# Expert stage of an encoder layer: u rows asked for one position ahead, interleaved with v rows; both halves of a quad's v products behind tiles 0, 1 and 4, 5

## The chip, the cores and the metric

The kernel runs on one core of one Trainium2 chip. The metric is the device time of one execution in microseconds, the median of several runs. The core has TensorE (PE, with its weight loads PEld), VectorE (DVE), ScalarE (ACT), GpSimd (POOL), SyncE (SP) and 16 DMA engines that serve all queues. Inputs and outputs lie in device memory (HBM).

## What is computed

One layer of a bidirectional encoder on 1024 tokens of width 1024. A token-mixing half (attention and spatial gating) comes first, then a channel-mixing half, PEER: each token picks 128 of 16384 single-neuron experts (8 heads, top 16 each), and

```python
u = exp_u[ib]                                             # (tokens, 128, 1024)
a = jax.nn.gelu(jnp.einsum('td,ted->te', xb, u)) * gb
y = jnp.einsum('te,ted->td', a, exp_v[ib])                # 128 rows of v per token
```

The change lies in the last large stage, the one that forms y.

## The kernel before

The stage is the method `experts`. It treats the two halves of the 1024 tokens in two ways at once.

**Dense half (512 tokens).** All 16384 experts are applied, with the gate zero where an expert isn't chosen. The experts come in 128 chunks of 128; a loop over 128 *positions* j takes one chunk each (`chunk_of[j]`). For a chunk, SP loads the gates g, the hidden values h (or they are computed here, see `up`) and 128 rows of v (L2156, L2158, L2161). DVE multiplies g by h (L2346). ACT makes a high part of the product and of v (L2234, L2236), DVE the low parts (L2356 and L2360). PE works on a *pair* of positions: 8 output tiles n = 0 to 7, each 6 matmuls of 128x512 (three products for each of the two positions), and DVE adds each tile to y (`add`, L2323). A tile's PSUM bank is one of four, so tile n waits for the sum of tile n - 4. PE begins a pair when both positions' low parts are ready (`a_split`, `v_split`). In the first 88 positions, 64 chunks also need their hidden values: `up` runs 24 matmuls for one chunk, up(m + 3) behind tile 1 of each pair and up(m + 4) behind tile 6 of 20 of the 44 pairs, with its own split of u on ACT (L2217) and DVE (L2332).

**Gathered half (4 blocks of 128 tokens).** Here the chosen experts are fetched row by row. POOL issues indirect DMAs, each of 128 rows of 1024 f32 (512 KB). For the first factor, one DMA brings one u row for each of 128 tokens, into one of U_RING = 4 slots (L2184), and one custom DVE instruction multiplies it with the tokens and sums (`dot`, L2316). There are 352 such dots, DOTS = 4 for each of the first 88 positions. For the second factor, position m covers a *quad* of 4 tokens: four DMAs, one for each of LANES = 4, bring all 128 v rows of a token (L2194) into one of V_RING = 2 sets of slots. PE multiplies them with the gates held in `ex_spread` (`mix(m, half)`, L2420): 4 matmuls for each half of the width, 128x32 by 128x512. When half 1 is done, `mixed` counts up.

**What sets the order.** Each engine runs its own hand-written order. On POOL, for each position j: four u rows of position j (each waits until the slot's last dot is done: `dotted`), then a wait until `mixed` has reached j - 1, then four v lanes of position j:

```python
def fetch_v(m):
    r = m % V_RING
    if m >= V_RING:
        pool.wait_ge(mixed, m - V_RING + 1)
    for lane in range(LANES):
...
for j in range(C):
    if j < DOT_CHUNKS:
        for i in range(DOTS):
            fetch_u(EARLY_DOTS + j * DOTS + i)
    fetch_v(j)
```

On DVE, position j is: g*h, sum of a tile, dot 0, low part of the activations, sum, low part of v, dot 1, (low part of u), sum, dot 2, sum, dot 3. The sums of position j are those of the pair before: tiles 0 to 3 where j is even, 4 to 7 where it is odd. On PE, the four `mix` calls of a pair (positions m and m + 1, halves 0 and 1) stand behind tiles 1, 3, 5 and 7. All DMAs that POOL issues go through one queue in order (q0); SP and ACT have queues of their own. A few steps come once per 32 positions: `fetch_u` loads the next block's tokens on POOL's queue (L2183), and `row_out`, `turn_row` and `space` carry a block's result out of PSUM and its gates into `ex_spread`.

Of the kernel before, what the change touches and what calls it, by code (L numbers as in the profile page):

```python
# [49 lines left out]
EARLY_DOTS = 160  # L50
# [6 lines left out]
class Layer:  # L57
# [1995 lines left out]
    def experts(self, h2_hi, h2_lo, y, expert_at, expert_of, weight_of, dots):  # L2053
# [11 lines left out]
        DOTS = P // SEG  # L2065
        DOT_CHUNKS = (NG * P - EARLY_DOTS) // DOTS
        DOT_PAIRS = DOT_CHUNKS // 2
        FUSED = C - EARLY_UPS
        LANES = 4
        U_RING, V_RING = 4, 2  # L2070

        chunk_of, up_at, up_of = [], [], {}
        for pair in range(C // 2):
            twice = (pair + 1) * (FUSED - DOT_PAIRS) // DOT_PAIRS > pair * (FUSED - DOT_PAIRS) // DOT_PAIRS
            for i in range(2):
                j = 2 * pair + i
# [23 lines left out]
        v_got = [self.sem(f"ex_v_got{i}") for i in range(V_RING)]  # L2100
# [20 lines left out]
        with ExitStack() as c:  # L2121
# [5 lines left out]
            v_rows = self.sb(c, "ex_v_rows", [P, V_RING * LANES, D])  # L2127
# [19 lines left out]
            with nc.Block() as block:  # L2147
# [23 lines left out]
                @block.gpsimd  # L2171
                def _(pool):
                    every_v = a["peer_v"].rearrange("i j d -> (i j) d")
                    every_u = self.u_rows.rearrange("i j d -> (i j) d")

                    def fetch_u(n):
                        r, i = n % U_RING, n - EARLY_DOTS
                        if i >= U_RING:

                            pool.wait_ge(dotted, i - U_RING + 1)  # L2180
                        if n % P == U_RING - 1 and n // P > 1:

                            pool.dma_start(rows, self.h2_scr[n // P].rearrange("p (h n) -> p h n", h=2)).then_inc(next_rows_loaded, 16)  # L2183
                        pool.indirect_dma_start(u_rows[:, r], None, every_u,  # L2184
                                                bass.IndirectOffsetOnAxis(ap=expert_at[:, n // P, n % P:n % P + 1], axis=0)).then_inc(u_got[r], 16)

                    def fetch_v(m):
                        r = m % V_RING
                        if m >= V_RING:

                            pool.wait_ge(mixed, m - V_RING + 1)
                        for lane in range(LANES):
                            t = lane * 32 + m % 32
                            pool.indirect_dma_start(v_rows[:, r * LANES + lane], None, every_v,  # L2194
                                                    bass.IndirectOffsetOnAxis(ap=expert_of[:, m // 32, t:t + 1], axis=0)).then_inc(v_got[r], 16)

                    for j in range(C):
                        if j < DOT_CHUNKS:
                            for i in range(DOTS):
                                fetch_u(EARLY_DOTS + j * DOTS + i)  # L2200
                        fetch_v(j)

                @block.scalar
                def _(act):
# [170 lines left out]
                @block.tensor  # L2375
                def _(pe):
                    def turn_gates(b):
                        pe.wait_ge(gated, b + 1)
                        if b >= 2:

                            pe.wait_ge(row_placed, 2 * (b - 1))
                        pe.transpose(gate_ps, curve[:], self.ident[:]).then_inc(gates_turned, 1)

                    def turn_row(b, half):
                        pe.wait_ge(row_copied, b + 1)

                        pe.wait_ge(gates_held, min(b + 2, NG))
                        if half:

                            pe.wait_ge(row_placed, 2 * b + 1)  # L2390
                        for k in range(4):
                            at = (4 * half + k) * P
                            last = pe.transpose(turn_ps[:, k * P:(k + 1) * P], row[:, at:at + P], self.ident[:])
                        last.then_inc(row_turned, 1)

                    def up(j):
                        if j not in up_of:
                            return
                        i = up_of[j]
                        pe.wait_ge(u_split, i + 1)  # L2400
                        if i:

                            pe.wait_ge(gelu_done, i)
                        for k in range(KT):
                            part, cols = k // 4, slice((k % 4) * P, (k % 4 + 1) * P)
                            last = self.product3(pe, hid, u_hi[i % 2][:, part, cols], u_lo[i % 2][:, part, cols], h2_hi[:, k, 0:HALF], h2_lo[:, k, 0:HALF],
                                                 k == 0, k == KT - 1)
                        last.then_inc(hidden, 1)

                    def mix(m, half):  # L2410
                        r, at = m % V_RING, m % 32
                        if half == 0:
                            pe.wait_ge(v_got[r], 16 * LANES * (m // V_RING + 1))
                            if at % SPAN == 0:
                                pe.wait_ge(spaced, m // SPAN + 1)
                            if at == 0 and m:
                                pe.wait_ge(row_copied, m // 32)
                        for lane in range(LANES):
                            first = 32 * (lane * SPAN + at % SPAN) + on - at
                            last = pe.matmul(ps[lane * 32:(lane + 1) * 32, 4 + half], spread[:, first:first + 32],  # L2420
                                             v_rows[:, r * LANES + lane, half * HALF:(half + 1) * HALF], start=at == 0, stop=at == 31)
                        if half == 1:
                            last.then_inc(mixed, 1)
                    turn_gates(0)
                    for j in range(3):
                        up(j)
                    for pair in range(C // 2):
                        m = 2 * pair
                        if m and m % SEG == 0:
                            turn_gates(m // SEG)  # L2430
                        pe.wait_ge(a_split, 2 * pair + 2)
                        pe.wait_ge(v_split, 2 * pair + 2)
                        for n in range(KT):
                            d = slice(n * P, (n + 1) * P)
                            if pair or n >= 4:

                                pe.wait_ge(added, pair * KT + n - 3)
                            for i in range(2):
                                ring = (2 * pair + i) % 4
                                last = self.product3(pe, ps[:, n % 4], v_hi[:, ring, d], v_lo[:, ring, d], act_hi[ring], act_lo[ring],  # L2440
                                                     i == 0, i == 1)
                            last.then_inc(summed, 1)
                            if n % 4 == 0 and m and m % SEG == 0:
                                turn_row(m // SEG - 1, n // 4)
                            if n % 2:
                                mix(m + n // 4, n // 2 % 2)
                            if n == 1:
                                up(m + 3)
                            if n == 6:
                                up(m + 4)  # L2450
                    turn_row(NG - 1, 0)
                    turn_row(NG - 1, 1)
# [59 lines left out]
```

## Time and profile before

| | us |
|---|---|
| median of 3 runs | 5116.48 (5108.94 to 5135.47) |
| the profiled execution | 5122.61 |
| its span | 5121.0 |
| PE, DVE, ACT, POOL busy in the span | 3897.4, 3018.5, 1490.2, 1250.4 |
| stage `experts`, first to last g*h on DVE | 3291.86 to 5043.14 |

The profile's page gives busy times of engines, the span in 40 slices (128 us each) with the rate of the DMAs, and groups of instructions. "Idle before" names what ended the idle time of an engine; for POOL, "issue" is a fixed gap in which it waits for nothing that is shown. The granted clock of TensorE is given as a share of 2.4 GHz. In the timeline, PE's ends are modelled and overlap the next start, so start to start is the time that a matmul takes.

### The profile page before, as it was taken

How to read it: one execution, taken by the hardware profiler on the slowest of the kernel's cores; microseconds unless marked ns; L12 is line 12 of the kernel's file. 1: busy time of each engine (PE TensorE's matmuls, PEld its weight loads, DVE VectorE, ACT ScalarE, POOL GpSimd, SP SyncE). 2: the span in 40 equal slices, each digit the busy share in tenths (PEclk: the TensorE clock that was granted, in tenths of full speed). 3: DMA queues.
4: the chain of work that ended last, by engine and by line, in shares of the span. 5: the costliest groups of instructions: out<-in, count | busy, mean ns of one | idle time of the engine just before them, and what ended most of it. 6: DMA issues, size and time to landing. Idle time of an engine off the chain costs nothing. (4 is left out here: it accounts for less than half of the span.)

```text
span 5121.0 us, 51116 instructions
## 1 busy us (share of the span) xinstructions
PE 3897.4 (76%) x17580; PEld 2820.9 (55%) x17580; DVE 3018.5 (59%) x5900; ACT 1490.2 (29%) x2161; POOL 1250.4 (24%) x1080
## 2 busy tenths in 40 slices
PE   2899898798866977696654567587888788788886
PEld 1666665577655766585443455355555555555553
DVE  5666665112243322597999957766666666666555
ACT  3444443333332123212566521111111111111111
POOL 0000000000001000000000057655555555555442
PEclk9999897799987987798766688788889898998997
DMA  3000000577843346102322399999999999999996
GB/s 125 19 23 26 17 23 7 199 254 276 286 165 125 107 147 226 45 29 74 105 70 72 111 337 368 355 338 335 343 338 344 345 349 334 339 345 331 342 353 242
DMA packets 386986, 1058.67 MB, mean 207 GB/s; under 512 B 33776, under 2 KB 102768, under 8 KB 383600
## 3 DMA queue, kind: packets, MB, share of 16 engines
q0 software_dynamic: 153504, 567.35, 29.5%
q1 hardware_dynamic: 185568, 351.11, 20.3%
q10 hardware_dynamic: 47728, 137.91, 7.3%
q8 instruction: 96, 1.57, 0.1%
q14 instruction: 90, 0.74, 0.0%
HBM read 905.76 MB, written 150.47 MB: 206 GB/s over the span
## 5 line engine op out<-in xcount | busy, mean ns | idle before, releaser
L2194 POOL DMA_INDIRECT ex_v_rows<-peer_v_dram,expert_of x512 | 609.5, 1190 | 649.2 <-PE psum L2420 504.4
L2316 DVE CUSTOM_DVE_ANT_1 ex_u_rows<-ex_u_rows,y 128x1024 f32<-128x1024 f32 x352 | 428.5, 1218 | 498.1 <-DMA ex_u_rows<-u_rows_scratch,expert_at 480.5
L382 PE MATMUL psum<-in_hi,v_hi 128*128 128x512 f32 x1024 | 462.8, 452 | 278.1 <-DVE v_lo L2360 134.3
L382 PE MATMUL psum<-in_hi 128*128 128x512 f32 x1024 | 440.7, 430 | 99.3 <-DVE in_lo L1913 52.3
L382 PEld LDWEIGHTS psum<-in_hi,v_hi 128*128 128x128 f32 x1024 | 212.5, 208 | 504.1 <-issue 378.9
L2323 DVE TENSOR_TENSOR y<-y,psum 128x512 f32<-128x512 f32 x512 | 349.0, 682 | 169.6 <-PE psum L384 159.0
L383 PE MATMUL psum<-in_lo,v_hi 128*128 128x512 f32 x1024 | 434.1, 424 | 0.0
L384 PE MATMUL psum<-in_hi,v_lo 128*128 128x512 f32 x1024 | 432.8, 423 | 0.0
L383 PE MATMUL psum<-in_lo,in_hi 128*128 128x512 f32 x1024 | 423.6, 414 | 0.0
L384 PE MATMUL psum<-in_hi,in_lo 128*128 128x512 f32 x1024 | 422.7, 413 | 0.0
L2184 POOL DMA_INDIRECT ex_u_rows<-u_rows_scratch,expert_at x352 | 378.2, 1074 | 150.6 <-issue 103.7
L2234 ACT ACTIVATE in_hi<-g 128x512 fp32r<-128x512 f32 x128 | 80.9, 632 | 1115.1 <-DVE g L2346 1074.8
L1036 POOL DMA_DIRECT2D gates_ada<-w_adaT_dram x16 | 8.7, 543 | 1432.0 <-PEq L521 930.3
L382 PEld LDWEIGHTS psum<-in_hi 128*128 128x128 f32 x1024 | 207.8, 203 | 184.4 <-issue 77.2
L1763 POOL DMA_INDIRECT sc_cand<-u_rows_scratch,expert_at x108 | 145.4, 1346 | 661.2 <-DVE expert_of L1866 582.7
L2420 PE MATMUL psum<-ex_v_rows,ex_spread 128*32 128x512 f32 x2048 | 275.0, 609 | 38.7 <-DMA ex_v_rows<-peer_v_dram,expert_of 34.8
L2040 PE MATMUL psum<-sc_w_hi,sc_second 128*128 128x128 f16 x512 | 101.2, 287 | 228.9 <-DVE sc_second L1892 228.9
L384 PEld LDWEIGHTS psum<-in_hi,v_lo 128*128 128x128 f32 x1024 | 212.9, 208 | 51.6
L383 PEld LDWEIGHTS psum<-in_lo,v_hi 128*128 128x128 f32 x1024 | 214.6, 210 | 39.3
L384 PEld LDWEIGHTS psum<-in_hi,in_lo 128*128 128x128 f32 x1024 | 206.9, 202 | 46.8
L383 PEld LDWEIGHTS psum<-in_lo,in_hi 128*128 128x128 f32 x1024 | 207.5, 203 | 38.1
L382 PE MATMUL psum<-in_hi,front_w_hi_t 128*128 128x512 f32 x512 | 216.3, 422 | 15.4 <-DVE front_w_lo_t L479 15.4
(357 smaller groups left out, 8636.7 us busy)
## 6 DMA issues: line engine op xcount, KB each, us to landing
y<-peer_v_dram SPq DMA_DIRECT2D x128, 512.0 KB
front_r_in<-peer_uT_dram SPq DMA_DIRECT2D x96, 512.0 KB
u_rows_scratch<-front_r_out ACTq DMA_DIRECT2D x96, 512.0 KB, 3.8
sc_u_raw<-peer_uT_dram SPq DMA_DIRECT2D x64, 512.0 KB
route_scratch<-sc_stage SPq DMA_DIRECT2D x32, 1024.0 KB, 10.5
g<-route_scratch SPq DMA_DIRECT2D x128, 256.0 KB
front_w_raw<-w_in_dram SPq DMA_DIRECT2D x32, 512.0 KB, 6.2
gates_ada<-w_adaT_dram POOLq DMA_DIRECT2D x16, 1024.0 KB
```

The source lines that it names most:

```text
L382: pe.matmul(out, w_hi, x_hi, start=start, stop=False)
L383: pe.matmul(out, w_hi, x_lo, start=False, stop=False)
L384: return pe.matmul(out, w_lo, x_hi, start=False, stop=stop)
L1036: pool.dma_start(ada[:, s], a["w_adaT"][:, bass.ds(at[s], 2), :]).then_inc(ada_loaded[s], 16)
L1763: pool.indirect_dma_start(u_rows[r], None, every_u, bass.IndirectOffsetOnAxis(ap=expert_at[:, n // P, n % P:n % P + 1], axis=0)).then_inc( ...
L2040: pe.matmul(to, second[:, s, tok], w_hi[:, s, tok], start=True, stop=False)
L2184: pool.indirect_dma_start(u_rows[:, r], None, every_u, bass.IndirectOffsetOnAxis(ap=expert_at[:, n // P, n % P:n % P + 1], axis=0)).then_i ...
L2194: pool.indirect_dma_start(v_rows[:, r * LANES + lane], None, every_v, bass.IndirectOffsetOnAxis(ap=expert_of[:, m // 32, t:t + 1], axis=0) ...
L2234: act.activation(act_hi[ring], g[:, s], ACT.Copy).then_inc(a_hi_done, 1)
L2316: dve.tensor_tensor_reduce(out=halves(u_rows[:, r]), in0=halves(u_rows[:, r]), in1=rows, scale=1.0, scalar=0.0, op0=ALU.mult, op1=ALU.add, ...
L2323: dve.tensor_tensor(to, to, ps[:, n % 4], ALU.add).then_inc(added, 1)
L2420: last = pe.matmul(ps[lane * 32:(lane + 1) * 32, 4 + half], spread[:, first:first + 32], v_rows[:, r * LANES + lane, half * HALF:(half + 1 ...
```

## The change

Two edits. On POOL, the four u rows of position 0 are issued first; then, at position j, one u row of position j + 1 and one v lane of position j alternate. The wait for `mixed` stands before lane 0, behind the first u row. On PE, `mix(m, 0)` and `mix(m, 1)` stand behind tiles 0 and 1, `mix(m + 1, 0)` and `mix(m + 1, 1)` behind tiles 4 and 5.

```diff
-                    def fetch_v(m):
-                        r = m % V_RING
-                        if m >= V_RING:
+                    def fetch_v(m, lane):
+                        r, t = m % V_RING, lane * 32 + m % 32
+                        if lane == 0 and m >= V_RING:
 
                             pool.wait_ge(mixed, m - V_RING + 1)
-                        for lane in range(LANES):
-                            t = lane * 32 + m % 32
-                            pool.indirect_dma_start(v_rows[:, r * LANES + lane], None, every_v,
-                                                    bass.IndirectOffsetOnAxis(ap=expert_of[:, m // 32, t:t + 1], axis=0)).then_inc(v_got[r], 16)
-
+                        pool.indirect_dma_start(v_rows[:, r * LANES + lane], None, every_v,
+                                                bass.IndirectOffsetOnAxis(ap=expert_of[:, m // 32, t:t + 1], axis=0)).then_inc(v_got[r], 16)
+
+                    for i in range(DOTS):
+                        fetch_u(EARLY_DOTS + i)
                     for j in range(C):
-                        if j < DOT_CHUNKS:
-                            for i in range(DOTS):
-                                fetch_u(EARLY_DOTS + j * DOTS + i)
-                        fetch_v(j)
+
+                        for i in range(DOTS):
+                            if j + 1 < DOT_CHUNKS:
+                                fetch_u(EARLY_DOTS + (j + 1) * DOTS + i)
+                            fetch_v(j, i)
...
-                            if n % 2:
-                                mix(m + n // 4, n // 2 % 2)
+                            if n % 4 < 2:
+                                mix(m + n // 4, n % 4)
```

Sizes of the rings, the number and size of the DMAs and all arithmetic stay as they were.

## Rows read from the trace of the kernel before

**Rows 1.** The page: the span, and the rate of the DMAs by slice.

```profile
span 5121.0 us, 51116 instructions
...
GB/s 125 19 23 26 17 23 7 199 254 276 286 165 125 107 147 226 45 29 74 105 70 72 111 337 368 355 338 335 343 338 344 345 349 334 339 345 331 342 353 242
```

**Rows 2.** The timeline of DVE: g*h of positions 0, 88 and 127.

```profile
3291.86 0.63 DVE L2346 SCALAR_TENSOR_TENSOR g<-g,h 128x512 f32<-128x512 f32 x1
...
4689.23 0.68 DVE L2346 SCALAR_TENSOR_TENSOR g<-g,h 128x512 f32<-128x512 f32 x1
...
5043.14 0.68 DVE L2346 SCALAR_TENSOR_TENSOR g<-g,h 128x512 f32<-128x512 f32 x1
```

**Rows 3.** Windows: stretch, its us, busy by engine, PE clock, DMA share, GB/s.

```profile
3292.00:4689.00 1397.00, 1118.92 (x4996) 746.72 (x4995) 894.94 (x1375) 242.94 (x324) 807.89 (x698) 0.89 0.93 342
4689.00:5043.00 354.00, 317.28 (x1560) 187.24 (x1559) 198.47 (x276) 65.42 (x88) 165.66 (x152) 0.97 0.94 341
3089.00:3250.00 161.00, 113.83 (x408) 87.07 (x408) 123.56 (x194) 24.94 (x33) 122.79 (x88) 0.87 0.97 365
3905.00:3931.00 26.00, 15.77 (x63) 10.63 (x64) 17.78 (x29) 4.10 (x5) 17.99 (x15) 0.80 1.00 384
3931.00:3938.00 7.00, 7.00 (x34) 4.58 (x32) 7.00 (x12) 1.02 (x2) 1.96 (x3) 1.00 0.72 225
```

**Rows 4.** Waits from 3292 to 4689: us in total, times, longest.

```profile
DVE ex_u_rows L2316 <- DMA ex_u_rows<-u_rows_scratch,expert_at: 480.5, 85, 10.7
...
POOL ex_v_rows L2194 <- PE psum L2420: 348.0, 62, 9.4
```

**Rows 5.** Waits from 4689 to 5043, the same columns.

```profile
POOL ex_v_rows L2194 <- PE psum L2420: 151.2, 37, 10.6
...
PE psum L2420 <- DMA ex_v_rows<-peer_v_dram,expert_of: 32.8, 20, 2.6
```

**Rows 6.** Timeline, early part: two mixes on PE, and the v lane POOL issues next.

```profile
4081.89 1.06 PE L2420 MATMUL psum<-ex_v_rows,ex_spread 128*32 128x512 f32 x8
...
4091.25 1.07 PE L2420 MATMUL psum<-ex_v_rows,ex_spread 128*32 128x512 f32 x8
...
4092.62 0.94 POOL L2194 DMA_INDIRECT ex_v_rows<-peer_v_dram,expert_of  x1 [8.61 <-PE psum L2420]
```

**Rows 7.** Groups of instructions from 3292 to 5043: busy, mean ns, idle before.

```profile
L2194 POOL DMA_INDIRECT ex_v_rows<-peer_v_dram,expert_of x500 | 597.5, 1195 | 641.0 <-PE psum L2420 499.2 <-issue 140.5 <-remote 1.3
...
L2316 DVE CUSTOM_DVE_ANT_1 ex_u_rows<-ex_u_rows,y 128x1024 f32<-128x1024 f32 x352 | 428.5, 1218 | 498.1 <-DMA ex_u_rows<-u_rows_scratch,expert_at 480.5 <-DMA y<-token_rows_scratch 17.6
...
L2184 POOL DMA_INDIRECT ex_u_rows<-u_rows_scratch,expert_at x348 | 374.5, 1076 | 140.5 <-issue 102.8 <-DVE dots L2316 37.7
L2323 DVE TENSOR_TENSOR y<-y,psum 128x512 f32<-128x512 f32 x500 | 340.7, 681 | 154.4 <-PE psum L384 145.4 <-issue 5.9
...
L2360 DVE TENSOR_TENSOR v_lo<-y,v_hi 128x1024 fp32r<-128x1024 f32 x127 | 155.6, 1225 | 0.0
```

**Rows 8.** Timeline: a u row's issue on POOL, and the dot that waited for it.

```profile
3909.80 0.94 POOL L2184 DMA_INDIRECT ex_u_rows<-u_rows_scratch,expert_at  x1 [0.30 <-issue]
...
3915.84 1.23 DVE L2316 CUSTOM_DVE_ANT_1 ex_u_rows<-ex_u_rows,y 128x1024 f32<-128x1024 f32 x1 [5.95 <-DMA ex_u_rows<-u_rows_scratch,expert_at]
```

**Rows 9.** Timeline, late part: mixes on PE.

```profile
4805.74 1.07 PE L2420 MATMUL psum<-ex_v_rows,ex_spread 128*32 128x512 f32 x8
...
4809.70 1.06 PE L2420 MATMUL psum<-ex_v_rows,ex_spread 128*32 128x512 f32 x8
...
4819.69 1.07 PE L2420 MATMUL psum<-ex_v_rows,ex_spread 128*32 128x512 f32 x8 [2.02 <-DMA ex_v_rows<-peer_v_dram,expert_of]
```

**Rows 10.** Timeline, late part: the first and last of four v lanes on POOL.

```profile
4807.11 0.94 POOL L2194 DMA_INDIRECT ex_v_rows<-peer_v_dram,expert_of  x1 [6.08 <-PE psum L2420]
...
4810.84 1.60 POOL L2194 DMA_INDIRECT ex_v_rows<-peer_v_dram,expert_of  x1 [0.30 <-issue]
```

## The prediction

> **What bounds the kernel now.** The page first: of a span of 5121.0 us, the 13 full slices from 3328 us on all lie between 331 and 353 GB/s, whatever the engines do in them [rows 1]. That is the stage `experts`. Its length is read from DVE's g*h [rows 2]: positions 0 to 88 take 1397.4 us, so a pair takes 31.76 us (44 pairs, with u rows); positions 88 to 127 take 353.9 us, so a pair takes 18.15 us (19.5 pairs, v rows alone). The windows [rows 3] show what each pair costs each engine in the first part: PE 1118.92 / 44 = 25.4 us at a granted clock of 0.89, DVE 894.94 / 44 = 20.3 us, POOL 807.89 / 44 = 18.4 us and 16 gaps of 0.30 us [rows 8], 23.2 us. None fills 31.76. The DMA engines are busy 93%. They move 342 x 1397 / 44 = 10.86 MB a pair.
>
> But the rate isn't steady. From 3905 to 3931, where POOL's queue is fed all the time, it is 384 GB/s at a share of 1.00; in the 7 us behind that, 225 [rows 3]. The waits say why: POOL waits 348.0 us, 62 times, for a mix on PE before it may ask for v rows, while DVE waits 480.5 us for u rows that stand behind those v rows in the same queue [rows 4]. One case: a mix(m, 0) starts at 4081.89, mix(m, 1) only at 4091.25, since an `up` and two tiles (36 matmuls, 8.3 us, 0.231 us each) stand between; POOL idles 8.61 us and issues at 4092.62 [rows 6]. So the bound is DMA with holes that the order of PE's work makes.
>
> **Edit 1, mixes on PE.** Count and cost stay. Two tiles and a mix take 3.96 us, so a tile is (3.96 - 1.06) / 2 = 1.45 us [rows 9]. `mixed` for an even position now comes behind tile 1, not 3: two tiles and an `up` (24 x 0.231 = 5.5 us) earlier, 8.4 us. For an odd position, behind tile 5, not 7: 2.9 us earlier, 8.4 where the pair has a second `up` (20 of 44). POOL's waits average 348.0 / 62 = 5.6 us, so most of them end at once. The other side: mix(m, 0) needs its v rows one tile (1.45 us) earlier, and what is queued behind its wait on PE is tile 1 and up(m + 3). The gates in `ex_spread` are wanted a tile earlier too, 16 times: 0 to 16 x 1.45 = 23 us. I take 0: ACT is busy 242.94 of 1397 us [rows 3] and what it waits for, `mixed`, comes earlier by more.
>
> **Edit 2, POOL's order.** The same 864 DMAs on the same queue. A u row is asked for as soon as the dot of the position before frees its slot, so it has nearly a whole position (14.7 us) for the 5.1 us from the end of its issue to its dot [rows 8], and no longer stands behind a wait for `mixed` (three of four do, but behind a wait that edit 1 ends). The 480.5 us of DVE should fall to what the DMA rate itself makes. The price: v lane i of position j now stands behind u row i of position j + 1, hence behind dot i of position j. From the end of dot 3: u issue 0.30 + 1.08, v issue 0.30 + 1.20 [rows 7, 8], 2.9 us, and then the landing, 5.1 us for the u row above and 4819.69 - 4812.44 = 7.25 us for a v lane of the late part [rows 9, 10]: the last lane is there 8.0 to 10.2 us behind dot 3. PE wants it no sooner than g*h, two sums, a dot and two low parts of DVE's next position (3 x 0.68 + 1.22 + 0.68 + 1.23 = 5.2 us, the activations' low part taken as one sum [rows 7]) and tile 0, 6.6 us. So PE may wait up to 3.6 us at mix(m, 0). It has 29.4 - 25.4 = 4.0 us to spare in a pair of the length forecast below. I cost it at nothing; without that cover it is 44 x 3.6 = 158 us. Smaller matters: the token load on POOL's queue (17.6 us of DVE's wait in all now [rows 7]) waits for the same dot as before, bounds 0 and another 17.6, taken as 0; v lanes of position 0 start behind the first dots (up to 5.3 us late), and the last mix ends up to 2.9 us sooner: taken as 0 together.
>
> **POOL as a cover.** Just ahead of the stage, with DVE busy 77%, a gather holds POOL 122.79 / 88 = 1.40 us [rows 3], against 1.20 and 1.08 in the stage [rows 7]. With DVE busier after the change, 16 x (1.40 + 0.30) = 27.2 us a pair, still under 29.4, but the margin is thin.
>
> **The rate, and the sum.** What remains is the DMA rate. Bounds: 342 (nothing filled) and 384 (no hole, over 26 us). The longest fed stretch is 3089 to 3250, 365 GB/s at a share of 0.97; scaled to 1.00 it is 376 [rows 3]. I take 370, nearest to that row. First part: 31.76 x 342 / 370 = 29.36 us, 2.40 us less, x 44 = 106 us. Late part: the ring of v slots sets it now. From the end of one mix(m, 1), 0.3 us to the issue, 5.3 us for four lanes (4807.11 to 4812.44), 7.25 us to the landing: 12.9 us; the rest of the pair, 2 tiles and 2 mixes behind it, is 5.0 us, together 17.9 against 18.15 seen [rows 9, 10]; POOL waits 151.2 us for mixes here, and PE 32.8 us for v rows [rows 5]. With the change one tile less is outside the ring: 16.5 us. By rate it is 18.15 x 341 / 370 = 16.7 us, which ends last: 1.42 x 19.5 = 28 us. PE alone needs 4 x 3.96 = 15.8. Sum: 134 us. Profiled execution 5122.6 - 134 = 4989 us; the median of the runs lies 6.1 us below it, so **4983 us**.
>
> **Rival 1, a lower ceiling of the DMAs.** If the rate is set by the mix of row gathers and block loads of this stage, no long stretch of it will pass 353 GB/s, the best full late slice [rows 1]; then 31.76 x 342 / 353 = 30.77 (44 us) and 17.53 (12 us) give 5061 us. For it: 13 slices of such even height. Against it: 384 over 26 us inside the stage, and 365 over 161 us [rows 3]. The Trainium skill, DMA: Bandwidth & Descriptors (Where 436 GB/s comes from), says that transfers between HBM and SBUF are bound by about 358 GB/s for a core; by that figure the sum would be about 79 us and the time about 5037. The same page's measured section says that a core alone on its pair goes higher, and this trace, with 365 and 384, sides with that.
>
> **Rival 2, a new wait for the old.** v lanes behind the dots leave POOL idle as long as before, only for `dotted` instead of `mixed`; the holes move and the pair stays at 31.8 us: 5116 us. For it: POOL already waits 37.7 us for dots [rows 7]. Against: dots are late now because of the u rows, and these come a position ahead.
>
> **Rival 3, slower: the last v lane closes a loop.** Dot 3 of position m, issue of the last lane (2.9 us), landing L, then on PE mix, tile 1, mix, `up`, tile 2 (1.06 + 1.45 + 1.06 + 5.5 + 1.45 = 10.5 us), then DVE's third sum of position m + 2, dot 2, sum, dot 3 (3.8 us): 17.2 + L per pair. It decides only from L = 31.76 - 17.2 = 14.6 us on; now L is 5.1 to 7.25. A u row and a v lane are issued together behind each dot, so the queue before the last lane gets longer; with L = 17 the pair is 34.2 us, + 107 us, less 28 in the late part: 5195 us. Against it: L would have to double, and one lane is 512 KB, 1.4 us at 370 GB/s, so five more would have to stand before it.
>
> **How the numbers follow.** Forecast 0.58, rival 1 0.20, rival 2 0.13, rival 3 0.09. 0.5% is 26 us, about what a measurement of this kernel can tell from no change. The first two cases are faster: 0.78; the third is the same: 0.13; the last slower: 0.09. Range: the low end is 384 GB/s throughout (28.29 us, 153 us; 16.5 us by the ring, 32 us: 4931), with 16 us more for a PE clock that rises from 0.89; the high end takes in rival 1 and part of rival 2: 4915 to 5105.
>
> **What would show it.** Right: windows of both parts at 365 GB/s or more and a share over 0.97; 29 to 29.7 us between every second g*h; POOL's wait for L2420 well under 150 us in the first part; DVE's wait for u rows under 250 us; PE waiting for v rows at L2420 at most 3 us each time. Rival 1: shares near 1 and 350 to 358 GB/s. Rival 2: POOL's wait for dots over 250 us. Rival 3: PE's waits for v rows over 5 us each, and DVE waiting for PE at its sums. I am wrong altogether if the rate stays at 342 with POOL hardly waiting.

## The result, and the profile after

The changed kernel takes 4926.32 us (median of 4 runs, 4921.15 to 4932.57), against 5117.1 us before. The ratio is 0.9623, 95% interval 0.9595 to 0.9651: 3.8% faster, a gain of 191 us where 134 were forecast. The profiled execution took 4932.57 us. First the page of the changed kernel: its span, and the rate of the DMAs by slice.

```profile
span 4930.9 us, 51116 instructions
...
GB/s 130 20 20 26 24 17 11 126 247 250 295 290 103 102 78 207 158 55 21 82 116 100 59 92 353 370 355 386 383 384 396 386 397 378 402 390 382 373 374 248
```

Where the slices stood at 331 to 353 GB/s before [rows 1], they are at 373 to 402 now. The timeline of DVE has g*h of positions 0, 88 and 127 again:

```profile
3297.88 0.63 DVE L2347 SCALAR_TENSOR_TENSOR g<-g,h 128x512 f32<-128x512 f32 x1
...
4523.31 0.68 DVE L2347 SCALAR_TENSOR_TENSOR g<-g,h 128x512 f32<-128x512 f32 x1
...
4855.94 0.68 DVE L2347 SCALAR_TENSOR_TENSOR g<-g,h 128x512 f32<-128x512 f32 x1
```

Against [rows 2] the first part fell from 1397.4 to 1225.4 us, a pair from 31.76 to 27.85; the late part from 353.9 to 332.6, a pair from 18.15 to 17.06. That is 172 + 21 us; the stage began 6 us later and what follows position 127 took 3 us less. Together 190 us, the difference of the spans. The windows (stretch, its us, busy by engine, PE clock, DMA share, GB/s):

```profile
3298.00:4523.00 1225.00, 1081.30 (x4991) 708.77 (x4989) 899.46 (x1375) 243.18 (x324) 851.66 (x702) 0.93 1.01 388
4523.00:4856.00 333.00, 312.07 (x1567) 183.55 (x1568) 202.37 (x277) 65.42 (x88) 162.28 (x156) 0.99 0.99 370
3089.00:3250.00 161.00, 120.47 (x432) 92.70 (x432) 125.30 (x197) 25.89 (x34) 129.01 (x89) 0.86 0.99 374
```

Each engine's busy time in the first part is what it was within some 6% [rows 3]: POOL's rose from 807.89 to 851.66 us, and PE's fell from 1118.92 to 1081.30 us at a granted clock of 0.93, against 0.89. The DMA share went from 0.93 to 1.01. No work went away, only holes. Now the waits of the first part (us in total, times, longest):

```profile
DVE y L2324 <- PE psum L384: 244.7, 78, 6.0
...
POOL ex_u_rows L2184 <- DVE dots L2317: 173.2, 61, 12.6
...
PE psum L2421 <- DMA ex_v_rows<-peer_v_dram,expert_of: 131.3, 28, 9.2
...
DVE ex_u_rows L2317 <- DMA ex_u_rows<-u_rows_scratch,expert_at: 58.0, 50, 3.9
...
POOL ex_v_rows L2192 <- PE psum L2421: 17.0, 13, 2.0
```

and of the late part:

```profile
POOL ex_v_rows L2192 <- PE psum L2421: 131.0, 38, 6.3
...
PE psum L2421 <- DMA ex_v_rows<-peer_v_dram,expert_of: 21.9, 21, 3.0
```

Against [rows 4], POOL's wait for mixes fell from 348.0 to 17.0 us, and DVE's wait for u rows from 480.5 to 58.0. Three waits have come up: PE for v rows, 131.3 us, where the kernel before has none in this part; DVE behind it, which now waits 244.7 us for PE at its sums (1.0 before); and POOL for dots, 173.2 us (37.7 before). One such case in the timelines of POOL and PE:

```profile
3900.82 0.94 POOL L2184 DMA_INDIRECT ex_u_rows<-u_rows_scratch,expert_at  x1 [0.31 <-issue]
3902.07 1.44 POOL L2192 DMA_INDIRECT ex_v_rows<-peer_v_dram,expert_of  x1 [0.30 <-issue]
...
3912.92 1.94 PE L2421 MATMUL psum<-ex_v_rows,ex_spread 128*32 128x512 f32 x8 [6.21 <-DMA ex_v_rows<-peer_v_dram,expert_of]
```

The lane issued until 3903.51 is the fourth of its position. PE's wait for it ends at 3912.92, 9.4 us later; PE stands idle for 6.21 us with tile 1 and an `up` queued behind the mix. Over the 28 waits of the first part, the time from the end of the fourth lane's issue to the mix that waited for it is 5.8 to 10.5 us, 8.5 us on average.

### The profile page after: what moved, and what is told of

The parts are those of the page before. It is cut to its first block and busy times, and to the rows that moved or that the text cites. A ratio compares the mean times of both kernels' runs of the same rounds, so it can differ in the third digit from the quotient of the medians.

```text
span 4930.9 us, 51116 instructions
## 1 busy us (share of the span) xinstructions
PE 3863.2 (78%) x17580; PEld 2786.9 (57%) x17580; DVE 3026.2 (61%) x5900; ACT 1490.5 (30%) x2161; POOL 1288.2 (26%) x1080
## 5 line engine op out<-in xcount | busy, mean ns | idle before, releaser
L2192 POOL DMA_INDIRECT ex_v_rows<-peer_v_dram,expert_of x512 | 621.5, 1214 | 295.1 <-PE psum L2421 150.9
L2184 POOL DMA_INDIRECT ex_u_rows<-u_rows_scratch,expert_at x352 | 400.2, 1137 | 273.4 <-DVE dots L2317 173.2
L382 PE MATMUL psum<-in_hi,v_hi 128*128 128x512 f32 x1024 | 437.0, 427 | 10.5 <-DVE v_lo L2361 7.2
L2421 PE MATMUL psum<-ex_v_rows,ex_spread 128*32 128x512 f32 x2048 | 295.2, 651 | 155.6 <-DMA ex_v_rows<-peer_v_dram,expert_of 154.7
L383 PE MATMUL psum<-in_lo,v_hi 128*128 128x512 f32 x1024 | 411.1, 401 | 0.0
L384 PE MATMUL psum<-in_hi,v_lo 128*128 128x512 f32 x1024 | 409.6, 400 | 0.0
L382 PEld LDWEIGHTS psum<-in_hi,v_hi 128*128 128x128 f32 x1024 | 197.8, 193 | 244.3 <-issue 147.8
L384 PEld LDWEIGHTS psum<-in_hi,v_lo 128*128 128x128 f32 x1024 | 198.6, 194 | 45.6
L2040 PEld LDWEIGHTS psum<-sc_w_hi,sc_second 128*128 128x128 f16 x512 | 66.0, 131 | 276.1 <-DVE sc_second L1892 276.1
```

Source lines behind the costliest of these rows:

```text
L382: pe.matmul(out, w_hi, x_hi, start=start, stop=False)
L383: pe.matmul(out, w_hi, x_lo, start=False, stop=False)
L384: return pe.matmul(out, w_lo, x_hi, start=False, stop=stop)
L2040: pe.matmul(to, second[:, s, tok], w_hi[:, s, tok], start=True, stop=False)
L2184: pool.indirect_dma_start(u_rows[:, r], None, every_u, bass.IndirectOffsetOnAxis(ap=expert_at[:, n // P, n % P:n % P + 1], axis=0)).then_i ...
```

## Experiments

Ratios are against the kernel before, run on the same chip. A pair's length is read from g*h as above, in one profiled execution of each kernel. The experiments have labels, e1 to e15; "after" in their expectations is the changed kernel.

**The two edits apart.** e1 is the mix edit alone, on the kernel before:

```diff
-                            if n % 2:
-                                mix(m + n // 4, n // 2 % 2)
+                            if n % 4 < 2:
+                                mix(m + n // 4, n % 4)
```

> Only the new places of the mixes on PE; POOL's order as before. Theory A (the gain is holes in the DMA stream, made mostly by the late `mixed`): POOL's wait for mixes in the first part falls from 348 us to under 120, the rate rises to about 370 GB/s, the time falls by 100 to 140 us, 4980 to 5015 us; the late part has all of its gain, a pair of about 17.1 us. Theory B (u rows that stand behind v rows are the cause, whoever releases them): DVE's wait for u rows stays over 350 us and the time falls by 20 to 60 us, 5055 to 5095 us, the late part's 21 us most of it.

Measured: 4902.66 us, ratio 0.9572 (0.9540 to 0.9605). Windows of both parts, then waits of the first:

```profile
3293.00:4486.00 1193.00, 1086.19 (x4999) 709.40 (x4997) 897.73 (x1378) 243.12 (x324) 827.36 (x698) 0.94 1.03 401
4486.00:4829.00 343.00, 315.03 (x1560) 184.90 (x1561) 201.75 (x275) 65.41 (x88) 161.07 (x155) 0.98 0.95 352
```

```profile
DVE ex_u_rows L2316 <- DMA ex_u_rows<-u_rows_scratch,expert_at: 248.9, 81, 4.6
...
POOL ex_u_rows L2184 <- DVE dots L2316: 160.5, 138, 8.0
...
POOL ex_v_rows L2194 <- PE psum L2420: 45.8, 54, 1.6
```

The rate is 401 GB/s, a pair of the first part takes 27.10 us, and there is no wait of PE for v rows in the list. Theory A holds for the first part, and the gain is half again as large as it said; the late part has only half of its gain (17.60 us a pair, not 17.1). This edit alone wins 216 us, more than both together. The two ratio intervals overlap slightly, so the stage is the better witness: from g*h of position 0 to that of 127 it is 1535.9 us here and 1558.1 in the changed kernel. DVE still waits 248.9 us for u rows, four times as long as in the changed kernel, and the kernel is faster all the same: that wait isn't what bounds.

e2, the POOL edit alone, is the changed kernel with the old `mix` lines.

> Only POOL's new order; the mixes stay behind tiles 1, 3, 5, 7. Theory A: POOL still waits for `mixed` before lane 0 and now holds u rows 1 to 3 of the next position behind that wait too, yet they have a position to spare; 5050 to 5085 us, late part 18.1 us a pair as before. Theory B: nearly the whole gain of the first part without any of the late part's, 4945 to 4975 us.

Measured: 5038.01 us, 0.9840 (0.9795 to 0.9884), 12 us under the range of theory A, far from theory B. A pair of the first part takes 29.73 us, a late pair 18.28. Its window and waits of the first part:

```profile
3302.00:4610.00 1308.00, 1109.29 (x4998) 731.87 (x4996) 908.17 (x1376) 243.36 (x324) 827.00 (x702) 0.92 0.96 364
```

```profile
POOL ex_v_rows L2192 <- PE psum L2421: 265.6, 61, 9.1
...
PE psum L2421 <- DMA ex_v_rows<-peer_v_dram,expert_of: 165.8, 45, 6.9
```

So of the medians (before 5117 to 5119): mixes alone -216, POOL alone -81, both -191. The second edit, as it stands, is a gain only without the first.

**Release or need?** In the changed kernel the slots are both needed and released earlier. In e3, made from the changed kernel, the halves are side by side too, but behind tiles 2, 3 and 6, 7:

```diff
-                            if n % 4 < 2:
-                                mix(m + n // 4, n % 4)
+                            if n % 4 >= 2:
+                                mix(m + n // 4, n % 4 - 2)
```

> As after, but both halves side by side behind tiles 2, 3 and 6, 7, so that `mixed` comes as late as before while the v rows are needed later. If the earlier `mixed` is what counts (theory A), about e2's time, within 15 us, and a late pair near 18.1 us. If it is the pairing of the halves that counts (v slots held for a shorter stretch between half 0 and half 1), near the time of after, 4925 to 4950 us. In the late part the distance from the end of mix(m, 1) to mix(m + 2, 0) is 7 tiles and 2 mixes as in after, so the ring would allow 16.5 us there: by that working a late pair is 17.1 us, and 20 us of the gain remain.

Measured: 4919.13 us, 0.9599 (0.9568 to 0.9631), a pair of 27.91 us and a late one of 16.96. That is not e2's time but that of the changed kernel, which speaks against theory A as I had put it. The waits of the first part point at a reason:

```profile
POOL ex_v_rows L2192 <- PE psum L2421: 168.5, 53, 7.9
...
PE psum L2421 <- DMA ex_v_rows<-peer_v_dram,expert_of: 94.8, 38, 5.7
```

Under POOL's new order there are two losses, POOL's wait for the release and PE's wait for late v lanes (265.6 and 165.8 us in e2). Both are smaller here. A reading that fits, though e3 alone doesn't show it: half 0 behind tile 2 runs after up(m + 3), so PE has more to do before it needs the lanes; and as PE then waits less before half 1, the release comes sooner too. To see the release alone, e9 has the same places with POOL's order of before, where PE has no wait for v rows in the list of the first part:

> POOL's order of before; mixes side by side behind tiles 2, 3 and 6, 7. The slots are released at the same place of PE's program as before, only half 0 comes later. Theory A (the release is what makes the holes): POOL's wait for mixes stays over 300 us in the first part, 31 to 32 us a pair, and only the late part gains its 20 us: 5090 to 5110 us. Theory E (the first part gains when no `up` stands between the halves, for whatever reason, as e3 against e2 suggests with 119 us): 4900 to 4930 us.

Measured: 5093.86 us, 0.9949 (0.9931 to 0.9968). Windows, and POOL's wait in the first part:

```profile
3290.00:4690.00 1400.00, 1121.86 (x4997) 748.11 (x4996) 896.09 (x1376) 242.64 (x324) 812.25 (x698) 0.90 0.93 341
4690.00:5013.00 323.00, 308.49 (x1560) 180.80 (x1558) 195.46 (x277) 65.46 (x88) 165.88 (x152) 1.00 1.00 375
```

```profile
POOL ex_v_rows L2194 <- PE psum L2420: 350.4, 64, 9.4
```

Theory A: 31.81 us a pair as before, 341 GB/s against 342, the same wait, and only the late part gains (16.55 us, the shortest so far). With POOL's order of before it is the release that counts. e10, made from the kernel before, leaves the mixes behind tiles 1, 3, 5, 7 and moves what stood in front of the release:

```diff
-                            if n == 1:
+                            if n == 3:
                                 up(m + 3)
-                            if n == 6:
+                            if n == 7:
                                 up(m + 4)
```

> POOL's order and the mixes' tiles (1, 3, 5, 7) of before; only the two `up` calls move behind tiles 3 and 7, behind the mixes. The halves stay apart by a tile or two, the release comes 5.5 us earlier where an `up` stood between. Theory A: 5.5 of the 8.4 us of an even position are won, POOL's wait for mixes falls by 150 us or more, first part 28.5 to 29.5 us a pair, late part unchanged at 18.1: 5000 to 5030 us. Theory E gives about the same for the first part. If only halves side by side help: 5100 to 5120 us.

Measured: 4962.03 us, 0.9697 (0.9678 to 0.9716), 38 us under the range of theory A: 28.14 us a pair at 386 GB/s, the late part hardly changed (18.37). The windows' row and POOL's wait:

```profile
3275.00:4513.00 1238.00, 1082.69 (x4998) 723.83 (x4996) 896.03 (x1376) 243.52 (x324) 830.08 (x698) 0.93 1.00 386
```

```profile
POOL ex_v_rows L2194 <- PE psum L2420: 130.2, 76, 4.3
```

With every mix behind its old tile, the `up` calls out of the way win 161 us. The halves needn't be neighbours. This run alone doesn't part theories A and E, since the `up` no longer stands between the halves either; e9 does, and there the release, left late, kept the pair at 31.81 us.

**POOL's order.** With the mixes as in the changed kernel, three other orders. e4 has first four u rows of the next position, then four lanes:

```diff
-                        for i in range(DOTS):
-                            if j + 1 < DOT_CHUNKS:
-                                fetch_u(EARLY_DOTS + (j + 1) * DOTS + i)
-                            fetch_v(j, i)
+                        if j + 1 < DOT_CHUNKS:
+                            for i in range(DOTS):
+                                fetch_u(EARLY_DOTS + (j + 1) * DOTS + i)
+                        for i in range(DOTS):
+                            fetch_v(j, i)
```

> As after, but at each position first the four u rows of the next position, then the four v lanes, instead of one of each by turns. If the alternation matters (the last v lane only 2.9 us behind the last dot, the first ones earlier), all four lanes come behind dot 3, the last at least 3 x 1.5 us later, PE's wait for v rows grows from 136 us to over 250 and the time is 20 to 60 us over after, 4945 to 4985 us. If only asking ahead matters, within 10 us of 4926.

Measured: 5023.76 us, 0.9817 (0.9781 to 0.9852), about 97 us over the changed kernel, far more than expected; a pair takes 30.11 us. Waits of the first part:

```profile
POOL ex_u_rows L2184 <- DVE dots L2318: 350.6, 139, 12.4
...
PE psum L2422 <- DMA ex_v_rows<-peer_v_dram,expert_of: 211.3, 48, 8.8
```

All lanes now stand behind dot 3. POOL idles for dots as long as it once did for mixes, and PE waits for v rows 48 times in 44 pairs, as in rival 3's loop. e5 alternates, but with u rows of the same position (no four rows up front, `fetch_u(EARLY_DOTS + j * DOTS + i)` before `fetch_v(j, i)`):

> The new places of the mixes, and POOL alternates u row i and v lane i of the same position (not one ahead). Mix edit alone gave 4903 with u first and then v; after, which asks u one position ahead, 4926, with 131 us of PE waiting for v rows. Theory C (v lanes behind the dots of their own position are what POOL's edit costs): here v lane i of position j stands only behind dot i of position j - 1, so PE's wait for v rows is under 30 us, but u rows 1 to 3 come up to three lanes later than in the mix edit alone; 4900 to 4920 us. Theory D (the alternation is what costs, since it spreads the last v lane): 4920 to 4945 us with PE's wait for v rows over 80 us.

Measured: 5021.55 us, 0.9790 (0.9764 to 0.9817); both theories missed. A pair takes 30.01 us. Waits of the first part:

```profile
DVE ex_u_rows L2315 <- DMA ex_u_rows<-u_rows_scratch,expert_at: 368.2, 189, 6.1
...
POOL ex_v_rows L2192 <- PE psum L2419: 307.6, 82, 9.2
...
PE psum L382 <- DVE v_lo L2359: 172.2, 23, 11.1
```

PE has no wait for v rows in the list, as theory C has it, but u rows 1 to 3 are now behind the wait for `mixed` and needed at once; PE waits 172.2 us for DVE's low parts, and the release comes late with it. Of these orders, alternating pays only with the u rows ahead, and u rows ahead only with the alternation.

e7 is the changed kernel with the two calls of the inner loop exchanged, the v lane first:

> As after, but v lane i comes ahead of u row i of the next position, so it stands behind dot i - 1 and not dot i, and lane 0 behind no dot of its own position. Theory C (PE's wait for v rows, 131 us, comes of lanes behind dots): that wait falls under 60 us and the time to 4900 to 4915. But u row 0 of the next position is now behind the wait for `mixed`, as in e5: if that costs more, the time is over 4930 and DVE's wait for u rows is over 150 us instead of 58.

Measured: 4893.44 us, 0.9546 (0.9521 to 0.9571), clear of the changed kernel's interval; a pair takes 26.95 us. Waits of the first part:

```profile
DVE ex_u_rows L2317 <- DMA ex_u_rows<-u_rows_scratch,expert_at: 152.8, 112, 3.9
...
POOL ex_u_rows L2184 <- DVE dots L2317: 117.5, 84, 11.4
...
PE psum L2421 <- DMA ex_v_rows<-peer_v_dram,expert_of: 47.8, 26, 5.2
```

Theory C holds, with a time 7 us below its range: one place in the queue takes PE's wait from 131.3 to 47.8 us and 44 x 0.90 = 40 us off the first part. DVE's wait for u rows did pass the 150 us that was to go with a loss, and there was none.

**Is the rate the bound now?** The page of the mix-only kernel (e1) has this rate by slice (122.6 us each):

```profile
GB/s 131 20 20 26 21 20 11 112 252 258 287 298 112 94 77 208 169 56 21 82 116 70 64 118 315 380 356 404 402 400 403 399 398 401 403 402 365 371 336 256
```

The nine full slices of its first part are even, 398 to 404 GB/s; those of the changed kernel range from 378 to 402. e11 is the mix edit alone with less to load. It reads only the first two blocks of v for the dense half and leaves out the rest, and with them SP's and ACT's waits for those blocks:

```diff
-                        if j >= 2:
-                            sp.wait_ge(v_split, j - 1)
-                        sp.dma_start(v_raw[s], ...
+                        if j < 2:
+                            sp.dma_start(v_raw[s], ...
...
-                        act.wait_ge(v_loaded[s], 16 * (j // 2 + 1))
+                        act.wait_ge(v_loaded[s], 16)
```

> The mix edit alone, without the block loads of v for the dense half from position 2 on (the first two blocks are used again and again): 1.05 of 10.8 MB a pair less. It leaves that part of the input out. If the DMA rate is what bounds the first part now (399 GB/s at a share of 1.02), a pair falls from 27.1 us to 9.76 / 0.399 = 24.5 us and the time by 90 to 120 us, 4785 to 4815 us. If PE's order and its waits bound it (PE busy 91%), by less than 40 us. In the late part the ring of v slots bounds: no more than 20 us in either case.

Measured: 4818.86 us, 0.9415 (0.9388 to 0.9442). Windows of both parts:

```profile
3283.00:4423.00 1140.00, 1069.82 (x5008) 703.24 (x5011) 898.81 (x1378) 243.36 (x324) 848.48 (x698) 0.96 0.99 378
4423.00:4733.00 310.00, 306.45 (x1554) 181.42 (x1547) 201.89 (x276) 65.46 (x88) 161.60 (x155) 1.00 0.94 327
```

It falls between the two readings. A pair goes from 27.10 to 25.91 us, not to 24.5. So fewer bytes help, and with the even slices this speaks for the rate as the bound of the mix-only kernel's first part, but something else is at most 1.2 us behind it. PE, then busy 1069.82 / 1140 = 94%, is the nearest candidate; the DMA share is still 0.99 there, and no run separates the two. The late pair goes from 17.60 to 15.89, the 15.8 us of PE's own work that the prediction gave. That is 33 us where at most 20 were expected: the ring holds the landing of the lanes, which fewer bytes may shorten, so bytes and ring weren't apart as the expectation had them.

**Putting the parts together.** e12 has mixes behind tiles 0, 1 and 4, 5 up to position 87, behind 2, 3 and 6, 7 from there on, with POOL's order of before:

```diff
-                            if n % 2:
-                                mix(m + n // 4, n // 2 % 2)
+                            late = 2 if m >= DOT_CHUNKS else 0
+                            if late <= n % 4 < late + 2:
+                                mix(m + n // 4, n % 4 - late)
```

> POOL's order of before; mixes behind tiles 0, 1 and 4, 5 for positions 0 to 87, behind tiles 2, 3 and 6, 7 from 88 on. If the parts add up: first part 27.1 us a pair (as the mix edit alone), late part 16.6 us (as e9), 4883 us, 20 us under the mix edit alone. If e9's late part owes its speed to how it is entered, the late pair stays near 17.6 us and the time near 4903.

Measured: 4884.14 us, 0.9524 (0.9499 to 0.9550); 27.20 and 16.62 us a pair, as expected. e14 adds one u row ahead of the wait (`fetch_u(EARLY_DOTS)` up front, and `range(1, DOTS + (j + 1 < DOT_CHUNKS))` for the rows of a position):

> As the kernel with two places of the mixes, with only u row 0 of the next position asked for ahead of the wait for `mixed`: dot 0 stands before the low parts on which PE's next pair waits. If the DMA rate (401 GB/s, share 1.03) bounds the first part, nothing: within 8 us of the other. If PE's waits at the start of a pair still count, 10 to 25 us less. All four v lanes come behind dot 0 of their own position, which costs if PE then waits for v rows.

Measured: 4864.85 us (4857.05 to 4882.0), 0.9494 (0.9466 to 0.9521), the fastest of the kernels that compute all of y. But its first part is shorter by 4 us only (27.11 us a pair), the late one by 5 us (16.35), and in its profile the stage began 10 us sooner, in code that is the same. From g*h of position 0 to the end of the span it is 1588.2 us against 1597.1. That fits the rate as the bound of the first part, and by these traces 9 of the 19 us between the medians are all that can be owed to this edit. Last, e15, the v lane first with the two places:

> POOL's order with the v lane first, and the late mixes behind tiles 2, 3 and 6, 7. If both gains hold and add up: first part 26.95 us a pair, late part 16.4 to 16.6 instead of 17.1, 10 to 14 us under the v-first kernel (4893): 4879 to 4884 us. If the rate has nothing left and the late part depends on how it is entered: within 5 us of 4893.

Measured: 4877.39 us (4859.22 to 4883.88), 0.9514 (0.9492 to 0.9535); 26.99 and 16.44 us a pair, as expected, and a time 2 us under its range. Windows of both parts:

```profile
3288.00:4475.00 1187.00, 1074.76 (x5010) 705.28 (x5012) 904.25 (x1376) 243.25 (x324) 843.58 (x701) 0.96 1.02 402
4475.00:4796.00 321.00, 306.39 (x1550) 180.42 (x1549) 195.82 (x277) 65.44 (x88) 164.89 (x152) 1.00 1.00 378
```

The intervals of the last three kernels overlap; which of them is best isn't settled. All beat both given kernels.

## Why the prediction was right, and where it was off

**What bounds.** Right: holes in the DMA stream, made by the late `mixed`. e1 (the release earlier), e10 (an earlier release by another way) and e9 (the release left late) show it each from its own side.

**Edit 1.** The mechanism was right and its share too small in my telling, as I gave no sum for it apart. Alone it is worth 216 us. That PE's need one tile earlier would cost nothing holds with POOL's order of before: e1's first part has no wait of PE for v rows in its list.

**Edit 2.** Here is the step that failed: "I cost it at nothing". I had put PE's wait at up to 3.6 us a pair and let PE's spare time cover it. The last lane lands later than the 5.1 to 7.25 us that I read from the old trace: 9.4 us in the case shown, 8.5 on average. PE waits 131.3 us over 28 times, 4.7 us each and up to 9.2, where the prediction's own sign said at most 3. The spare time, 27.85 - 24.6 = 3.3 us a pair as measured, didn't cover all of it: in e7 that wait is 83.5 us less and the first part 40 us shorter. The other half of the step, that DVE's wait for u rows should fall, came true (480.5 to 58.0), but beside edit 1 it was worth little: the first part is 33 us longer than e1's as the edit stands, and 7 us shorter with e7's order. I took it for part of the bound, and it was mostly where the missing bandwidth showed.

**POOL as a cover.** It held: 851.66 / 702 = 1.21 us a request, not the 1.40 allowed for; with the gaps 24.2 us a pair.

**The rate.** The term that was mis-sized, and most of the 57 us by which the gain was larger. I took 370 GB/s, with 384 as the far bound since that was the best 26 us of the old trace. The stage runs at 388 and, in the mix-only kernel, at 401 for 1193 us. A stretch inside a trace that starves again and again isn't a ceiling. By the sum's own formula, 388 gives 31.76 x (1 - 342 / 388) x 44 = 166 us for the first part, against 106 in the sum; 172 were measured. (Rate and length come from one trace, so this says only that the bytes stayed the same.) The late part was put at 16.7 us a pair and took 17.06, though the rate was the 370 GB/s of the sum: 156 of POOL's requests and not 152 fall in it, 2 MB more. The signs that named rates and shares came true; the 29 to 29.7 us for a pair did not.

**Luck in the range.** The low end, 4915, was worked out from 384 GB/s throughout. Edit 1 alone went past it, to 4902.66 us at 401 GB/s. What brought the changed kernel back to 4926 is the cost of edit 2, which stood in the sum at nothing. So two errors partly cancel: a rate put too low, and a wait put at nothing. The 16 us that the low end allowed for a faster clock can't be told apart; the clock rose from 0.89 to 0.93, while PE was busy 88% of the first part.

**Rival 1** fell: the full slices of the first part are at 378 or more. By this, the 358 GB/s that the Trainium skill gives as a core's share (DMA: Bandwidth & Descriptors, Where 436 GB/s comes from) bounds nothing here; its measured section, by which a core alone on its pair goes higher, agrees with 401. **Rival 2** fell for the whole. POOL does wait 173.2 us for dots, but so it does, 160.5 us, in the faster e1 with the order of before, so that wait alone says little; in e4, with 350.6, half of the gain is gone. **Rival 3** didn't close in every pair (28 waits in 44), but it was nearer than the prediction put it, and its signs are there: waits of PE over 5 us and DVE waiting for PE at its sums. Its threshold of 14.6 us belongs to the old pair. For a pair of 27.85 us it is 27.85 - 17.2 = 10.7 us (an estimate from the prediction's own terms), and landings reached 10.5. The stall that it names at mix(m, 0) is the cost of edit 2.

What stays open: the late part of the mix-only kernel takes 17.60 us a pair and that of the changed kernel 17.06, though from position 88 on both run the same orders. So do e4, e5 and e7, with 17.48, 17.02 and 17.11. How the part is entered may matter, or it is the spread of single executions; no run tells. Places 2, 3 and 6, 7 are better there in all five kernels that have them (16.35 to 16.96), and e12 shows that this doesn't hang on a slow first part. Why is not known, as the ring's distance is the same 7 tiles and 2 mixes.

## What to carry to other kernels

With a ring of few slots and one in-order queue of transfers, find the instruction that frees a slot and ask what stands before it that needn't; moving 36 matmuls out of the way was worth more than asking for the u rows earlier. An engine's long wait for data can name the place where bandwidth is missing, and not the cause. When two edits aim at the same holes, time them apart: the second may cost.

## What was not expected

In e1 and e15 a rate of 401 and 402 GB/s, at a share of 1.03 and 1.02, held for over 1100 us of 4 KB rows gathered from two tables beside block loads, 10% over the best long stretch of the old trace. And the earlier stages, whose code is the same in all these kernels, put the stage's first g*h anywhere from 3275 to 3302 us, so differences under 20 us between two of these kernels are better read from the stage than from the whole time.
